# MLP up products by seven of eight block products, in turn with the preceding part's down products

## The chip, the cores and the metric

The kernel runs on one core of one Trainium2 chip. The metric is device time in microseconds of that core; a span is the time from the first to the last instruction of one profiled execution. A core has TensorE (matrix products into PSUM, eight banks of 512 float32 columns per partition), VectorE (DVE), ScalarE (ACT), GpSimd (POOL) and SyncE (SP, which here only starts DMAs). Each engine works through a queue of its own; they meet at semaphores.

## The reference

Two blocks follow each other on one sequence of 512 tokens with 1024 features, in float32. The first block has two layers, each a mixer (layer 0 a gated delta rule beside a short convolution, layer 1 a sparse attention) and an MLP:

```python
def squared_relu_mlp(h, w_up, w_down):
    return jnp.square(jax.nn.relu(h @ w_up)) @ w_down
...
    for layer in range(DEPTH):
        h = rms_norm(x, mix_norm[layer])
        ...
        x = x + squared_relu_mlp(rms_norm(x, mlp_norm[layer]), w_up[layer], w_down[layer])
    return rms_norm(x, final_norm)
```

`w_up` is 1024 x 4096, `w_down` 4096 x 1024. The second block (two layers of latent attention beside a Fourier branch) has no MLP. The change touches the two MLPs and what leads into them.

## The kernel before

**Layout.** Activations stand feature-major: a tile is 128 features (partitions) x 512 tokens; `x` has KT = 8 of them. A product keeps a 128 x 128 weight tile in TensorE and streams the tokens.

**Three passes.** To keep float32 precision, each operand is split into a high part (rounded to fp32r) and a low part (the rest), and `three` (L758) forms w_hi x_lo + w_lo x_hi + w_hi x_hi in PSUM. Each pass loads its weights anew. `gemm` (L764) runs 8 input tiles x 3 passes = 24 matmuls for one output tile of 128 x 512 in the MLP.

**Weights.** `stream_of` lays all weights out as 312 blocks of eight 128 x 128 tiles, in the order of use. SP loads block b into `raw[b % 3]` once POOL has finished the low part of block b - 3 (L2693 to L2699). ACT makes `w_hi` (`weights`, L1407 to L1416) once TensorE has used block b - 3, POOL makes `w_lo` (L2709), and TensorE waits for `w_lo_ready`. ACT's copies stand in its queue between its other work: each step of the program first calls `weights(block + 2)`. `plan_core` (L321) walks through the program once and gives every product its block, PSUM bank and use number, and every split its number; all engines wait by these numbers.

**MLP.** Four parts of 1024 hidden features. In each, eight up products (L831 to L837); for each, DVE takes relu times the root of the norm into `relu` (L2082), ACT squares it into `stage` (L1530) and makes `a_hi`, DVE makes `a_lo` (L2032). Then eight down products (L839), each added to `x` by DVE (`add_to_x`, L2074). Products turn through banks 0 to 3.

**Into the MLP.** The mixer's output products come first, eight tiles of `x`: of 12 matmuls each in layer 0 (blocks of two tiles), of 24 in layer 1. Per tile DVE adds it to `x`; ACT makes `h_hi` (L1493) and its square (L1489); DVE makes `h_lo` (L2038) and adds the square to the norm sum (L2053) (`sums_before_norm` L2062, `products_before_norm` L1509). The first up product waits for each input tile by itself. The norm sum goes through TensorE (`norm_sum`, L819) after that product, and ACT forms the root with Ln and Exp (`norm_root`, L1502), which only the relu needs.

## Time and profile before

| what | us |
|---|---|
| median of 3 runs | 2103.3 |
| lowest and highest of the 3 | 2093.99, 2109.73 |
| span of the profiled execution | 2099.7 |

Of the profiled execution the page gives the span alone; the time of a run has some microseconds around its span. Busy time of an engine is the union of its instructions. The marked time of a matmul holds its way through the array as well, so matmuls overlap in the record and the rate is read from their starts. Weight loads are a row of their own, PEld. In a row of a group, "idle before" is what the engine stood still ahead of its instructions, and the name after the arrow is what ended it. The record's clock row gives the granted clock as 1.00 of full speed for the span.

### The profile page before, as it was taken

The page shows a single profiled execution, that of the slowest core. Times are in us where ns is not written, and L with a number is a line of the kernel's source. Part 1 is how long each engine was busy: PE and PEld are TensorE (multiplying, and loading weights), DVE is VectorE, ACT ScalarE, POOL GpSimd, SP SyncE. Part 2 cuts the span into 40 slices and gives each one's busy share as a digit, 9 for nine tenths or more (in the row PEclk, how much of TensorE's full clock was granted, in tenths as well). Part 3 has the DMA queues.
Part 4 walks back from the last instruction along what each step waited for, and adds up shares of the span by engine and source line. Part 5 has one row for each costly group of instructions (what it writes and reads, how often), then busy time and mean ns, then how long its engine had stood idle before and what let it go on. Part 6 is the DMA issues. An engine that isn't in the chain of part 4 may idle for free.

```text
span 2099.7 us, 28844 instructions
## 1 busy us (share of the span) xinstructions
PE 2076.6 (99%) x11148; PEld 1645.5 (78%) x11148; DVE 947.6 (45%) x1431; ACT 933.3 (44%) x1477; POOL 759.2 (36%) x316
## 2 busy tenths in 40 slices
PE   8999999999999999999999999999999999999999
PEld 5777788888888886668888888778788887877887
DVE  7875552112137256765211212667733354773331
ACT  7642453323236326774322324556742344765231
POOL 3332144444444630003444444344034443402443
PEclk9999999999999999999999999999999999999999
DMA  4442133333332431002333333232022333201232
GB/s 155 134 123 70 45 104 99 92 101 91 94 99 88 146 96 31 2 14 92 100 91 101 91 101 101 74 97 81 12 81 90 91 93 94 85 22 61 91 100 81
DMA packets 62710, 178.96 MB, mean 85 GB/s; under 512 B 17776, under 2 KB 18160, under 8 KB 62592
## 3 DMA queue, kind: packets, MB, share of 16 engines
q1 hardware_dynamic: 47600, 168.04, 26.3%
q10 hardware_dynamic: 14992, 9.22, 1.6%
q8 instruction: 89, 1.46, 0.3%
q14 instruction: 29, 0.24, 0.0%
HBM read 171.97 MB, written 3.70 MB: 84 GB/s over the span
## 4 chain that ended last, share of the span: by engine, by line
issue 48%; PE 34%; POOL 16%; ACT 1%; POOLq 0%; DMA 0%; SPq 0%; DVE 0%
POOL w_lo L2709 16%; PE banks L760 9%; PE banks L762 9%; PE banks L761 9%; PE banks L1282 1%; PE banks L1295 1%; PE banks L1267 1%; PE banks L811 1%; PE banks L1273 1%; PE banks L1239 0%; DMA x<-in_x 0%; PE banks L1330 0%; POOLq L2715 0%; POOLq L2717 0%; PE banks L1331 0%
## 5 line engine op out<-in xcount | busy, mean ns | idle before, releaser
L2709 POOL TENSOR_TENSOR w_lo<-raw,w_hi 128x1024 fp32r<-128x1024 f32 (+1 forms) x312 | 759.0, 2434 | 1322.8 <-ACT w_hi L1415 1322.7
L760 PE MATMUL banks<-h_lo,w_hi 128*128 128x512 f32 (+1 forms) x1408 | 567.0, 403 | 9.3 <-POOL w_lo L2709 9.3
L762 PE MATMUL banks<-h_hi,w_hi 128*128 128x512 f32 (+1 forms) x1408 | 554.7, 394 | 0.0
L761 PE MATMUL banks<-h_hi,w_lo 128*128 128x512 f32 (+1 forms) x1408 | 551.5, 392 | 0.0
L1415 ACT ACTIVATE w_hi<-raw 128x1024 fp32r<-128x1024 f32 (+1 forms) x312 | 327.9, 1051 | 489.4 <-PE banks L762 456.5
L760 PEld LDWEIGHTS banks<-h_lo,w_hi 128*128 128x128 f32 (+1 forms) x1408 | 264.4, 188 | 73.8 <-POOL w_lo L2709 8.7
L761 PEld LDWEIGHTS banks<-h_hi,w_lo 128*128 128x128 f32 (+1 forms) x1408 | 264.5, 188 | 62.2 <-issue 4.8
L762 PEld LDWEIGHTS banks<-h_hi,w_hi 128*128 128x128 f32 (+1 forms) x1408 | 264.3, 188 | 60.7 <-issue 0.7
L760 PE MATMUL banks<-a_lo,w_hi 128*128 128x512 f32 x768 | 304.5, 397 | 0.0
L762 PE MATMUL banks<-a_hi,w_hi 128*128 128x512 f32 x768 | 301.6, 393 | 0.0
L761 PE MATMUL banks<-a_hi,w_lo 128*128 128x512 f32 x768 | 299.8, 390 | 0.0
L2074 DVE TENSOR_TENSOR x<-x,banks 128x512 f32<-128x512 f32 x104 | 71.4, 687 | 341.0 <-PE banks L762 341.0
L762 PEld LDWEIGHTS banks<-a_hi,w_hi 128*128 128x128 f32 x768 | 144.3, 188 | 33.4
L761 PEld LDWEIGHTS banks<-a_hi,w_lo 128*128 128x128 f32 x768 | 144.4, 188 | 33.0 <-issue 1.0
L760 PEld LDWEIGHTS banks<-a_lo,w_hi 128*128 128x128 f32 x768 | 144.5, 188 | 31.3 <-issue 1.3
L2082 DVE SCALAR_TENSOR_TENSOR relu<-banks,norm 128x512 f32<-128x512 f32 x64 | 44.3, 692 | 270.5 <-PE banks L762 259.8
L1530 ACT ACTIVATE stage<-relu 128x512 f32<-128x512 f32 x64 | 40.5, 632 | 208.7 <-DVE relu L2082 208.7
L2053 DVE TENSOR_TENSOR norm<-norm,sq 128x512 f32<-128x512 f32 x49 | 85.7, 1749 | 2.5 <-ACT sq L1489 1.2
L1973 ACT ACTIVATE sig<-sig,params 128x512 f32<-128x512 f32 x32 | 23.2, 726 | 140.6 <-DVE sig L2635 140.6
L2635 DVE TENSOR_TENSOR sig<-banks,norm 128x512 f32<-128x512 f32 x32 | 22.1, 692 | 111.6 <-PE banks L762 111.6
L1821 ACT ACTIVATE prob<-banks,nb 128x128 f32<-128x128 f32 (+3 forms) x128 | 66.2, 534 | 1.4 <-DVE nb L2452 1.4
L2032 DVE TENSOR_TENSOR a_lo<-stage,a_hi 128x512 fp32r<-128x512 f32 x84 | 61.6, 733 | 7.5 <-ACT a_hi L1478 7.3
(365 smaller groups left out, 2466.5 us busy)
## 6 DMA issues: line engine op xcount, KB each, us to landing
raw<-in_weights SPq DMA_DIRECT2D x311, 512.0 KB, 3.6
x<-in_x SPq DMA_DIRECT2D x4, 512.0 KB, 6.2
AT<-row_dram ACTq DMA_DIRECT2D x4, 512.0 KB, 7.6
out<-x SPq DMA_DIRECT2D x8, 256.0 KB, 2.6
eg<-row_dram ACTq DMA_DIRECT2D x8, 128.0 KB, 3.3
phase<-in_phase ACTq DMA_DIRECT2D x1, 706.0 KB, 4.9
phase<-in_phase ACTq DMA_DIRECT2D x1, 704.0 KB, 4.2
ld_dram<-Ld ACTq DMA_DIRECT2D x1, 512.0 KB, 5.4
```

The costliest lines, as they stand in the source:

```text
L760: mm(out, w_hi, x_lo, start=first, stop=False)
L761: mm(out, w_lo, x_hi, start=False, stop=False)
L762: return mm(out, w_hi, x_hi, start=False, stop=last)
L1415: f(c.w_hi[:, b % RING, 0:n], c.raw[:, b % RING, 0:n], ACT.Copy).then_inc(c.w_hi_ready, 1)
L1530: step(f(c.stage[:, split[key] % 3, :], c.relu[:, i % 2, :], ACT.Square))
L1821: ins = f(c.prob[:, i % 4, s, e], c.pairs[bank[key][0] // 2][:, s, e], ACT.Exp, bias=c.nb[:, i % 4, m:m + 1], accum_out=c.nb[:, i % 4, 4 + ...
L1973: f(gate, gate, ACT.Sigmoid, bias=pa["merge"][:, at:at + 1]).then_inc(c.sig_ready, 1)
L2032: tt_op(dst, stage(key, False), hi.bitcast(F32), ALU.subtract).then_inc(c.split_lo, 1)
L2053: tt_op(c.norm[:, slot, :], c.norm[:, slot, :], c.sq[:, i % 2, :], ALU.add).then_inc(c.norm_sum, 1)
L2074: tt_op(c.x[:, m, :], c.x[:, m, :], out[:, :], ALU.add).then_inc(release(key), 1)
L2082: stt(c.relu[:, i % 2, :], product(key)[:, :], 0.0, r, ALU.max, ALU.mult).then_inc(release(key), 1)
L2709: return nc.gpsimd.tensor_tensor(c.w_lo[:, slot, 0:n], c.raw[:, slot, 0:n], c.w_hi[:, slot, 0:n].bitcast(F32), ALU.subtract)
```

## The change

An up product of a 256-feature group `g` (of 512 in a part; eight parts now) is a matrix of 2 x 2 blocks times the input's 2 x 2 blocks (two feature tiles x two halves of the tokens). With sums of weight blocks and sums of input blocks made beforehand, seven block products take the place of eight, and seven to nine additions put the result together. So:

- A weight block holds one group's eight tiles for four input tiles (two pairs). ACT copies its W21 quarter to PSUM bank 4 (`w21`), DVE forms four sums in banks 4 and 5 (`weight_sums`), ACT makes their high part (`sums_hi`), DVE their low part (`weight_sums_lo`). W21's own high and low parts are not made; ACT's and POOL's work on such a block is three quarters.
- On the way in, input tiles go in pairs: ACT writes the gained tile to bank 6, DVE forms four sums in banks 6 and 7, and high and low parts follow (`pair_hi`, `input_sums`, `input_sums_hi`, `pair_lo`, `input_sums_lo`).
- `seven` issues per block 7 products x 2 pairs x 3 passes = 42 matmuls of 256 columns; two blocks make a group.
- ACT copies the first product (`first`), DVE adds the products up in PSUM, takes relu there, ACT squares from PSUM, DVE takes the low part from PSUM. `relu` is gone.
- The order on TensorE is: two up blocks, then (from the second part on) four down products of the preceding part, of 12 matmuls each, in banks 6 and 7 by turns. Each down product is added to `x`, now 64 per MLP.
- The loops of SP and POOL over the blocks are written out.

```diff
-FF_PARTS = 4
+FF_PARTS = 8
...
+    def by_pairs(w):
+        for first in range(0, w.shape[0] // P, 4):
+            for out, into in ((1, 0), (0, 0), (0, 1), (1, 1)):
+                for k in (first, first + 2):
+                    yield w[(k + into) * P:(k + into + 1) * P, out * P:(out + 1) * P]
+        for part in range(FF_PARTS + 1):
+            for g in range(2):
+                if part < FF_PARTS:
+                    add(by_pairs(up[:, (2 * part + g) * SUM_BLOCK:(2 * part + g + 1) * SUM_BLOCK]))
+                if part:
+                    add(out_major(down[(part - 1) * T:part * T, g * T:(g + 1) * T]))
...
+SEVEN = [("p1", W_11, X_11), ("p2", W_12, X_21), ("p6", W_S2, X_T2), ("p3", W_S4, X_22), ("p7", W_S3, X_T3),
+         ("p5", W_S1, X_T1), ("p4", W_22, X_T4)]
+SUM_BANKS, INPUT_BANKS, DOWN_BANKS = (4, 5), (6, 7), (6, 7)
...
+    def seven(layer, part, g, half, beside_products=None):
+        key, first = ("up", layer, part, g), part == g == 0
+        b = block[key][0] + half
+        i_sum = sum_blocks.index(b)
+        pe.wait_ge(c.w_lo_ready, b + 1)
+        pe.wait_ge(c.s_lo_ready, i_sum + 1)
...
+        for n, (_, w, x) in enumerate(SEVEN):
+            bnk, use, _ = bank[(*key, n // 2)]
...
+                if part and n % 4 == 0:
+                    before = (part, 0) if g else (part - 1, part > 1)
+                    pe.wait_ge(c.split_lo, split[("a", layer, before[0], 2 * before[1] + n // 4)] + 1)
+            if n == 2 and beside_products:
+                pe.wait_ge(c.split_lo, split[("ht", 2 * layer + 1, PAIRS - 1)] + 1)
+                beside_products()
+            for k in range(2):
+                i = 2 * half + k
+                if first:
+                    pe.wait_ge(c.split_lo, split[("ht" if x > X_22 else "hx", 2 * layer + 1, i)] + 1)
...
+                x_hi, x_lo = c.hs_hi[:, i, x, :], c.hs_lo[:, i, x, :]
+                mm(out, w_hi, x_lo, start=half == k == n % 2 == 0, stop=False, skip_group_check=True)
+                mm(out, w_lo, x_hi, start=False, stop=False, skip_group_check=True)
+                ins = mm(out, w_hi, x_hi, start=False, stop=half == k == 1, skip_group_check=True)
+            if n == len(SEVEN) - 1:
+                ins.then_inc(c.block_used, 1)
+            elif half and n % 2:
+                ins.then_inc(c.bank_filled[bnk], 1)
...
+    def down(layer, part, g):
+        if g == 0:
+            pe.wait_ge(c.split_lo, split[("a", layer, part, NT - 1)] + 1)
+        x_hi, x_lo = [tiles(t, NT, part % 2 * NT) for t in (c.a_hi, c.a_lo)]
+        for m in range(NT * g, NT * g + NT):
+            gemm(("down", layer, part, m), x_hi, x_lo, tile0=m % 2 * NT)
...
+        for part in range(FF_PARTS + 1):
+            for g in range(2):
+                if part < FF_PARTS:
+                    seven(layer, part, g, 0)
+                    seven(layer, part, g, 1, (lambda: norm_sum(2 * layer + 1)) if part == g == 0 else None)
+                if part:
+                    down(layer, part - 1, g)
...
+            if b in sums:
+                w21(b)
+                sums_hi(b)
+            cols = slice(SUM_BLOCK if b in sums else 0, n)
+            f(c.w_hi[:, b % RING, cols], c.raw[:, b % RING, cols], ACT.Copy).then_inc(c.w_hi_ready, 1)
...
+        if i:
+            act.wait_ge(c.s_lo_ready, i)
...
+        f(c.psum[SUM_BANKS[0]][:, 0:SUM_BLOCK], c.raw[:, b % RING, 0:SUM_BLOCK], ACT.Copy).then_inc(c.w21_ready, 1)
...
+        act.wait_ge(c.weight_sums, i + 1)
+        if i > 1:
+            act.wait_ge(c.block_used, sums[i - 2] + 1)
+        f(c.w_hi_s[:, i % 2, :], c.pairs[SUM_BANKS[0] // 2][:, :, :].rearrange("p b t -> p (b t)"), ACT.Copy).then_inc(c.s_hi_ready, 1)
...
+    def pair_hi(n, k):
+        x_final(act, c, bank, n, k)
+        i, gain = k // 2, norm_gain(c, pa, n, k)
+        if k % 2:
+            f(c.hs_hi[:, i, X_21:X_22 + 1, :].rearrange("p b t -> p (b t)"), c.x[:, k, :], ACT.Copy, scale=gain).then_inc(c.split_hi, 1)
+        else:
+            f(c.hs_hi[:, i, X_11, :], c.x[:, k, 0:HALF], ACT.Copy, scale=gain)
+            if i:
+                act.wait_ge(c.split_lo, split[("ht", n, i - 1)] + 1)
+            else:
...
+            f(c.psum[INPUT_BANKS[0]][:, :], c.x[:, k, :], ACT.Copy, scale=gain).then_inc(c.gained, 1)
+        norm_square(n, k)
+    def input_sums_hi(n, i):
+        act.wait_ge(c.t_ready, (n // 2) * PAIRS + i + 1)
+        f(c.hs_hi[:, i, X_T2:X_T3 + 1, :].rearrange("p b t -> p (b t)"),
+          c.pairs[INPUT_BANKS[0] // 2][:, :, :].rearrange("p b t -> p (b t)"), ACT.Copy).then_inc(c.split_hi, 1)
...
+        for m in range(KT):
+            passed(*key, m)
+            if m % 2 == 0 and m:
+                pair_hi(n, m - 1)
+                input_sums_hi(n, m // 2 - 1)
+            elif m:
+                pair_hi(n, m - 1)
+        pair_hi(n, KT - 1)
+        input_sums_hi(n, PAIRS - 1)
...
+        for n, ((part, g), ahead) in enumerate(up_cycles()):
+            key, after = ("up", layer, part, g), block[("up", layer, *ahead)][0] if ahead else None
+            down = block[("down", layer, part - 1, NT * g)][0] if part else None
+            if part:
+                weights(down)
+            if ahead:
+                w21(after)
+            if n == 0:
+                norm_root(2 * layer + 1)
+            if part:
+                weights(down + 1)
+            if ahead:
+                sums_hi(after)
+            f(c.first[:, n % 2, :], filled((*key, 0))[:, 0:HALF], ACT.Copy).then_inc(c.first_ready, 1)
+            if ahead:
+                w21(after + 1)
+                weights(after)
+            for i in range(2):
+                m, y = 2 * g + i, c.psum[bank[(*key, 2 * i)][0]]
+                act.wait_ge(c.relu_ready, (layer * FF_PARTS + part) * NT + m + 1)
+                f(c.a_hi[:, part % 2 * NT + m, :], y[:, :], ACT.Square)
+                f(y[:, :], y[:, :], ACT.Square).then_inc(c.split_hi, 1)
+            if ahead:
+                sums_hi(after + 1)
+                weights(after + 1)
+        products_before_norm((2, "final")[layer], "down", layer, FF_PARTS - 1)
...
+    def weight_sums(b):
...
+        dve.wait_ge(c.w21_ready, i + 1)
+        tt_op(s3, w11, s1, ALU.subtract)
+        first = marked(tt_op(s1, s1, w22, ALU.add))
+        after(first)
+        second = marked(tt_op(s2, s1, w11, ALU.subtract))
+        after(second)
+        tt_op(s4, w12, s2, ALU.subtract).then_inc(c.weight_sums, 1)
+    def weight_sums_lo(b):
+        i = sums.index(b)
+        dve.wait_ge(c.s_hi_ready, i + 1)
+        tt_op(c.w_lo_s[:, i % 2, :], c.pairs[SUM_BANKS[0] // 2][:, :, :].rearrange("p b t -> p (b t)"),
+              c.w_hi_s[:, i % 2, :].bitcast(F32), ALU.subtract).then_inc(c.s_lo_ready, 1)
...
+    def input_sums(n, i):
...
+        dve.wait_ge(c.gained, (n // 2) * PAIRS + i + 1)
+        t1 = marked(stt(d[:, left], x1[:, right], g1, b[:, left], ALU.mult, ALU.subtract))
+        stt(d[:, right], x2[:, right], g2, b[:, right], ALU.mult, ALU.subtract)
+        after(t1)
+        t2 = marked(stt(b[:, left], x2[:, right], g2, d[:, left], ALU.mult, ALU.subtract))
+        after(t2)
+        stt(b[:, right], x2[:, left], g2, b[:, left], ALU.mult, ALU.subtract).then_inc(c.t_ready, 1)
+    def pair_lo(n, i):
...
+            ALU.mult, ALU.subtract)
+        hi_part, lo_part = [t[:, i, X_21:X_22 + 1, :].rearrange("p b t -> p (b t)") for t in (c.hs_hi, c.hs_lo)]
+        stt(lo_part, c.x[:, 2 * i + 1, :], norm_gain(c, pa, n, 2 * i + 1), hi_part.bitcast(F32), ALU.mult, ALU.subtract)\
+            .then_inc(c.split_lo, 1)
+    def input_sums_lo(n, i):
...
+        tt_op(lo_part, c.pairs[INPUT_BANKS[0] // 2][:, :, :].rearrange("p b t -> p (b t)"), hi_part.bitcast(F32), ALU.subtract)\
+            .then_inc(c.split_lo, 1)
...
+    def sums_before_pairs(n, *key):
+        for m in range(KT):
+            b = block[(*key, m)][1] + 2
+            if b in sums and b > prepared:
+                weight_sums(b)
+                weight_sums_lo(b)
+                prepared = b
+            add_to_x((*key, m), m)
+            if m:
+                norm_add(n, m)
+            if m % 2:
+                input_sums(n, m // 2)
+            elif m:
+                pair_lo(n, m // 2 - 1)
+                input_sums_lo(n, m // 2 - 1)
+        norm_add(n, KT)
+        pair_lo(n, PAIRS - 1)
+        input_sums_lo(n, PAIRS - 1)
...
+        left, right = slice(0, HALF), slice(HALF, T)
+        for n, ((part, g), ahead) in enumerate(up_cycles()):
+            key, b = ("up", layer, part, g), block[("up", layer, *ahead)][0] if ahead else None
...
+            if ahead:
+                weight_sums(b)
+                weight_sums_lo(b)
+            dve.wait_ge(c.first_ready, (layer * FF_PARTS + part) * 2 + g + 1)
+            tt_op(bank_0[:, left], bank_0[:, right], first, ALU.add)
+            filled((*key, 1))
+            u2_done = marked(tt_op(u2, bank_1[:, left], first, ALU.add))
+            after(u2_done)
+            filled((*key, 2))
+            u3_done = marked(tt_op(u3, bank_2[:, left], u2, ALU.add))
+            u4_done = marked(tt_op(u4, bank_2[:, right], u2, ALU.add))
+            after(u3_done)
+            tt_op(bank_2[:, right], bank_2[:, right], u3, ALU.add)
+            after(u4_done)
+            tt_op(bank_0[:, right], bank_1[:, right], u4, ALU.add).then_inc(release((*key, 1)), 1)
+            dve.wait_ge(c.block_used, block[key][0] + 2)
+            tt_op(bank_2[:, left], bank_3[:, left], u3, ALU.add).then_inc(release((*key, 3)), 1)
+            if n == 0:
+                r = root(2 * layer + 1)
+            read((*key, 1))
+            stt(bank_0[:, :], bank_0[:, :], 0.0, r, ALU.max, ALU.mult).then_inc(c.relu_ready, 1)
+            read((*key, 3))
+            stt(bank_2[:, :], bank_2[:, :], 0.0, r, ALU.max, ALU.mult).then_inc(c.relu_ready, 1)
+            if part:
+                add_to_x(("down", layer, part - 1, NT * g), NT * g)
+            if ahead:
+                weight_sums(b + 1)
+            for i in range(2):
+                m, a = 2 * g + i, ("a", layer, part, 2 * g + i)
+                dve.wait_ge(c.split_hi, split[a] + 1)
+                at = part % 2 * NT + m
+                tt_op(c.a_lo[:, at, :], c.psum[bank[(*key, 2 * i)][0]][:, :], c.a_hi[:, at, :].bitcast(F32), ALU.subtract)\
+                    .then_inc(c.split_lo, 1)
+            if ahead:
+                weight_sums_lo(b + 1)
+            if part:
+                for m in range(NT * g + 1, NT * g + NT):
+                    add_to_x(("down", layer, part - 1, m), m)
+        sums_before_norm(next_norm, "down", layer, FF_PARTS - 1)
...
+            for b in range(n_blocks):
                 pool.wait_ge(c.w_hi_ready, b + 1)
+                low_part(b % RING, SUM_BLOCK if b in sums else 0, TILES * (P if b else AB_ROWS)).then_inc(c.w_lo_ready, 1)
```

The rest of the diff places the new tensors and semaphores and passes `sums`, the list of the blocks with sums, to the engines' programs. `up_banks` gives a group banks 0 to 3, and 6, 1, 7, 3 to the second group of the first part.

## Rows read from the trace of the kernel before

**Rows 1.** The page: busy time, share of the span and instructions of each engine

```profile
PE 2076.6 (99%) x11148; PEld 1645.5 (78%) x11148; DVE 947.6 (45%) x1431; ACT 933.3 (44%) x1477; POOL 759.2 (36%) x316
```

**Rows 2.** The waits: engine and line that waited, for whom; us, times, longest

```profile
PE banks L760 <- POOL w_lo L2709: 9.3, 2, 8.3
```

**Rows 3.** The timeline in an up product of MLP 0: start us, us, engine, line

```profile
500.25 0.39 PE L760 MATMUL banks<-h_lo,w_hi 128*128 128x512 f32 x1
500.26 0.19 PEld L761 LDWEIGHTS banks<-h_hi,w_lo 128*128 128x128 f32 x1
...
505.06 0.39 PE L760 MATMUL banks<-h_lo,w_hi 128*128 128x512 f32 x1
```

**Rows 4.** The timeline of transposes of 128 columns: matmuls, and their weight loads

```profile
1882.74 1.09 PE L1282 MATMUL banks<-common,prob 128*128 128x128 f32 x8
...
1882.74 0.85 PEld L1282 LDWEIGHTS banks<-common,prob 128*128 128x128 f32 x8 [0.37 <-issue]
```

**Rows 5.** The timeline of the compression products, 320 and 160 columns in turn

```profile
686.33 0.36 PE L1069 MATMUL banks<-kc,w_hi 128*128 128x320 f32 x1
...
686.52 0.25 PE L1071 MATMUL banks<-kc,w_lo 128*128 128x160 f32 x1
686.52 0.19 PEld L1069 LDWEIGHTS banks<-kc,w_hi 128*128 128x128 f32 x1
686.61 0.35 PE L1069 MATMUL banks<-kc,w_hi 128*128 128x320 f32 x1
...
687.68 0.35 PE L1069 MATMUL banks<-kc,w_hi 128*128 128x320 f32 x1
```

**Rows 6.** Groups by line and form: count | busy us, mean ns | idle before, releaser

```profile
L2074 DVE TENSOR_TENSOR x<-x,banks 128x512 f32<-128x512 f32 x104 | 71.4, 687 | 341.0 <-PE banks L762 341.0
...
L2599 DVE TENSOR_REDUCE nb<-banks 128x2 f32<-128x1024 f32 x32 | 39.1, 1221 | 13.4 <-PE banks L1273 13.4
...
L2621 DVE TENSOR_TENSOR d_lo<-banks,d_hi 128x256 fp32r<-128x256 f32 x16 | 6.6, 423 | 2.6 <-ACT d_hi L1962 2.5
...
L1814 ACT ACTIVATE probT<-banks 128x1024 f32<-128x1024 f32 x24 | 24.6, 1025 | 15.5 <-PE banks L1172 15.5
...
L1962 ACT ACTIVATE d_hi<-banks 128x256 fp32r<-128x256 f32 x16 | 6.1, 382 | 3.7 <-PE banks L1333 2.8 <-PE banks L1331 0.5
...
L2709 POOL TENSOR_TENSOR w_lo<-raw,w_hi 128x1024 fp32r<-128x1024 f32 x311 | 757.8, 2438 | 1316.2 <-ACT w_hi L1415 1316.1
```

**Rows 7.** The timeline of DVE, and one row of POOL, at the entry to MLP 0

```profile
277.81 0.69 DVE L2074 TENSOR_TENSOR x<-x,banks 128x512 f32<-128x512 f32 x1 [2.06 <-PE banks L762]
278.41 0.75 DVE L2038 SCALAR_TENSOR_TENSOR h_lo<-x,params,h_hi 128x512 fp32r<-128x512 f32 x1
...
284.56 2.90 DVE L2053 TENSOR_TENSOR norm<-norm,sq 128x512 f32<-128x512 f32 x1
...
295.20 0.68 DVE L2074 TENSOR_TENSOR x<-x,banks 128x512 f32<-128x512 f32 x1
...
297.06 0.74 DVE L2038 SCALAR_TENSOR_TENSOR h_lo<-x,params,h_hi 128x512 fp32r<-128x512 f32 x1
...
284.50 2.42 POOL L2709 TENSOR_TENSOR w_lo<-raw,w_hi 128x1024 fp32r<-128x1024 f32 x1 [3.08 <-ACT w_hi L1415]
```

**Rows 8.** The timeline of ACT at the entry to MLP 0: the root of the norm

```profile
298.12 1.28 ACT L1505 ACT_TABLE_LOAD   x1
...
302.64 0.63 ACT L1507 ACTIVATE norm<-norm 128x512 f32<-128x512 f32 x1
```

**Rows 9.** TensorE's first matmuls (timeline), and the window over them (busy, PEclk, DMA, GB/s)

```profile
8.31 0.65 PE L760 MATMUL banks<-h_lo,w_hi 128*40 128x512 f32 x1 [8.31 <-POOL w_lo L2709]
...
11.25 0.39 PE L761 MATMUL banks<-h_hi,w_lo 128*40 128x512 f32 x1
11.49 0.40 PE L762 MATMUL banks<-h_hi,w_hi 128*40 128x512 f32 x1
...
9.50:12.00 2.50, 2.50 (x9) 1.12 (x8) 2.48 (x5) 2.49 (x5) 0.00 (x0) 1.00 1.03 414
```

196 lines of the change are left out of this document (120 added, 76 removed).

## The prediction

> **What bounds the kernel now.** I read the busy times first: the matmuls cover 2076.6 of 2099.7 us, and VectorE (DVE), ScalarE (ACT) and GpSimd (POOL) are each under half busy [rows 1]. TensorE waited for another engine for only 9.3 us in two places, 8.3 of them at the start [rows 2]. Busy TensorE time overlaps, so the rate comes from the timeline: between 500.25 and 505.06 us lie 21 matmuls of 512 columns, 0.229 us each, each with its own weight load of 0.19 us beside it [rows 3]. The kernel is a stream of such pairs, and time goes only if the stream gets shorter and nothing opens a hole in it.
>
> **What the change does to the stream.** Up products before: 2 layers x 32 tiles x 8 x 3 = 1536 matmuls x 0.229 = 351.7 us. After: 2 layers x 16 (part, g) x 2 blocks x 7 x 2 x 3 = 2688 matmuls of 256 columns. The columns fall by an eighth, the matmuls rise by three quarters. The break-even is 351.7 / 2688 = 0.131 us a matmul. The down products stay 1536 matmuls.
>
> No row has a 256-column fp32r stream, so I bound it. From 512 columns: 512 / 2.4 = 213, so each matmul pays 16 ns besides its columns; 256 / 2.4 + 16 = 123 ns. The load alone is no longer than that: eight transposes of 128 columns, each with a full load, take (1.09 - 0.28) / 7 = 0.116 us each, and their loads come every (0.85 - 0.14) / 7 = 0.10 us [rows 4]; I take 0.11, between them, as the lower bound. The upper one is the compression stage, where matmuls of 320 and 160 columns alternate: five pairs from 686.33 to 687.68 take 0.270 each [rows 5]. That is 35 ns a matmul over its columns, so 142 ns at 256. But those rows also say where the excess sits: the load for the matmul after the short one starts at 686.52, with the short one, and the matmul it serves ends at 686.96, so it began near 686.96 - 0.18 - 0.13 = 686.65, 0.125 after its load began (0.18 is what a 512-column matmul's 0.39 has over its columns [rows 3]). A 256-column stream gives its load just that time. I take 0.124: 2688 x 0.124 = 333.3 us, a gain of 18.4. Ends: 0.11 gives 56 us gained, 0.142 gives 30 us lost.
>
> The page "TensorE: Matmul & The Clock Gate" of the Trainium skill (Back-to-back issue gap) has N / 2.4 + 2.5 ns, 109 ns at 256 columns and 216 at 512; at 512 the trace has 229 [rows 3], so the trace disagrees. By the page the up stream would be 293 us, 40 less than I take.
>
> **In a steady cycle.** A cycle is seven-product blocks U0, U1 (42 x 0.124 = 5.2 each) and four down products of 12 x 0.229 = 2.75. Durations I use: DVE on PSUM 0.69 for 512 columns, 0.42 for 256, 1.22 for 1024 (the nearest row is a reduction); ACT 1.03 for 1024, 0.38 for 256, and so 0.81 for 768; POOL 2.44 a full block, so 1.8 for three quarters [rows 6]. Queued work starts about 0.09 before the end of its forerunner (277.81 + 0.69, next at 278.41 [rows 7]). The DVE work of a cycle is then some 14 of 21.5 us, ACT 10, POOL 8: no bound. The tight place is bank 7, between down product m1 and m3. DVE may begin add(m0) 2.98 us into the down products (2.75 + 0.18 + hop), and has queued before add(m1): add 0.6, four sums 1.65 (two wait for their forerunner), two a_lo 1.2, low part of the sums 1.15, add 0.69: it frees the bank at 8.3, and TensorE wants it at 8.25. With a hop, 0.13 us lost x 28 cycles = 3.6 us. Range 0 to 0.6 a cycle (0 to 17 us). ACT's copy of the sums lies beside the a_lo pair. The weight DMAs keep their size and count and their wait for w_lo; SP and POOL queues are in the same block order. Nothing of this is worth time. The waits that are new: ACT's sums_hi for weight_sums, with w_hi, squares and `first` behind it; DVE's low part for that copy, with the adds, and so banks 6 and 7, behind it; TensorE for the low sums, made 5 us or more ahead here.
>
> **Entering MLP 0.** Before, each output product (2.75 us) asks DVE for an add, a low half and a norm add. The last add starts at 295.20, the last low half at 297.06, and TensorE, done at about 294.1, takes h tile by tile and loses nothing [rows 7]. After, the pairs come in turn through one pair of PSUM banks (6, 7). Per pair DVE has: 2 adds 1.2, 2 norm adds 1.2, four input sums 1.6, pair_lo 0.4 + 1.2, the low part of the sums 1.15: 6.8 us against 5.5 of TensorE. To that come operations with two SBUF inputs (norm_add, pair_lo) that meet a POOL block: one took 2.90 instead of 0.68 beside a POOL block begun at 284.50 [rows 7]. And two weight_sums + low parts, in which DVE waits for ACT's copy between: 3.9 each; and ACT's gained copy of a pair, which waits for the pair before. Stepping through both queues from add(m1) at 277.81: input sums of pair 0 end at 280.2, its low parts at 284.8 (with 0.7 for a meeting with POOL). norm_add(3) waits until 286.2, for ACT's square, which stands behind the gained copy, and that waits for the low part of pair 0. Input sums of pair 1 end at 288.4, the weight sums of the first up block at 290.1, ACT's copy at 291.2, their low part at 292.4, add(m4) at 293.0, norm_add, behind POOL's block, at 294.6, pair_lo at 296.2, the low part of pair 1 at 297.3. The same round takes pair 2 to 308.7 and 309.9 (low weights of the second block at 306.5), and pair 3 to 315.8 and 317. TensorE has 3 matmuls after 294.1, goes on at 296.2, ends the first block at 301, has 3 matmuls after 308.7 and goes on at 315.8. Unhindered it would stand there at 294.1 + 5.2 + 0.4 = 299.7. Loss 16.0 us; 8 if POOL and ACT never stand in the way (only the 6.8 - 5.5 per pair and the two sums), 22 if every such meeting costs.
>
> **Entering MLP 1.** Output products take 5.5 us, so DVE is near level until the sixth. Sums for the second block can start only after it, and the chain behind them (sums with copy 3.8, add 0.6, norm_add, input sums, norm_add, pair_lo) makes pair 3 ready 10.3 us after the last product; TensorE wants it at 5.4. Loss 4.9 (0 to 8).
>
> **First blocks of each MLP.** ACT has norm_root ahead of sums_hi(after). Ln and Exp, each with a table load of 1.28, take from 298.12 to 303.27 before, beside full up tiles [rows 8]. After, the square sum comes in the second block, and behind the Exp stand sums_hi 1.03, DVE's low part 1.15, w21 0.38, w_hi 0.81, POOL 1.8: block 3 is ready 4.6 us after block 2 ends. With no down products between, the next three blocks miss by 0.9, 0.6 and 1.7 (relu, sums, ACT copy, POOL are 5.5 to 7 us in series behind a 5.2 us block). 7.8 x 2 layers = 15.6 us (8 to 22).
>
> **The clock.** After the 8.3 us wait at the start, seven steps between matmuls of 512 columns take 8.31 to 11.25, 0.42 us each, the next takes 0.24 [rows 9]: 512 / 1.2 GHz is 0.43, so this is the lower of the clock's two levels, though the granted clock of the stretch is given as 1.00. It cost some 1.3 us. For holes of 4 to 7 us I take 3 us in all (0 to 8).
>
> **Leaving an MLP.** Its last eight products are 2.75 instead of 5.5 us. That is what layer 0's output products were before, and there TensorE lost nothing [rows 7]: 0.
>
> **Sum.** -18.4 + 3.6 + 16.0 + 4.9 + 15.6 + 3.0 = +24.7 on the span of 2099.7 = 2124.4. The median of the runs, 2103.3, is 3.6 above that span: 2128.
>
> **Rivals.**
> A, at the entries the pairs come in time: DVE gets through a pair in the 5.5 us of TensorE, since it does not stand behind POOL and ACT as I step it. The holes of both entries and their clock loss go: 2128 - 16.0 - 4.9 - 3.0 = 2104, no change. It is not slower from the point where all holes together stay under the 18.4 us of the stream. For it: DVE idles 2.06 us before the add at 277.81 [rows 7], and every engine but TensorE is under half busy [rows 1]. Against: the chain is serial through ACT and one PSUM pair.
> B, the weight load paces the stream at 0.11: 2128 - 38 = 2090, and with A 2066. For it speak the transposes [rows 4], against it the 16 ns that every 512-column matmul pays although its load is long done [rows 3]. The page's rule above gives nearly this.
> C, 256 columns behave as the mixed pairs [rows 5], 0.142 each: 18 ns x 2688 = 48 us more, 2176.
> D, bank 7 is late by 0.6 us or more in each of the 28 cycles: 13 us more or over, 2141. The point from which it decides: DVE's queue between add(m0) and add(m1) over 5.5 us.
> E, the change saves no TensorE time at all, since the interval is 0.131: 2146.
>
> **Chances.** Forecast 0.50 (its own range 2112 to 2143), A 0.19, B 0.05, C 0.07, D 0.12, E 0.07. A measurement of this kernel can tell about 1% (21 us) from no change. Slower by over 1% (above 2124) takes 0.28 of the forecast's 0.50 and C, D, E: 0.54. Faster by over 1% (under 2082) needs B and A together, or the other holes small as well as A's: 0.07. Between: 0.39. The range leaves out B and half of C: 2098 to 2160.
>
> **What would show it.** Right: 256-column matmuls start 0.122 to 0.126 apart inside a block; TensorE idle of 12 to 18 us around the second up block of layer 0, waiting for DVE hs_lo; a wait of some 5 us for POOL w_lo at the third block of each layer; DVE busy about 1280 us (14 us in 32 cycles and some 40 at the entries, for the 135 of relu, a_lo and adds). Wrong: an interval of 0.13 or more, or under 0.118; TensorE without holes at both entries; down products that wait for a bank by more than 0.5 us in each cycle.

## The result, and the profile after

The kernel after takes 2120.21 us (median of 4 runs, 2119.11 to 2122.73), the kernel before 2102.25 (4 runs): a ratio of 1.0088, 95% interval 1.0061 to 1.0114, 18 us slower. The profiled execution has a span of 2117.6 us against 2099.7. The prediction of 2128 us was 8 us high, on the right side, and inside its range; of its steps some were right, one was right in size but put the wait at the wrong place, and the gain of the stream was put at little more than half of the true one.

The page of the kernel after, its busy time and the slices of TensorE and its clock:

```profile
PE 2059.5 (97%) x12300; PEld 1683.4 (79%) x12300; DVE 1233.6 (58%) x2079; ACT 1013.9 (48%) x1653; POOL 722.3 (34%) x316
...
PE   8999978999999999999899999999999999999999
...
PEclk9999989999999999999899999999999999999999
```

Against [rows 1], TensorE is busy for 17 us less with 1152 matmuls more: the work did become cheaper. DVE gained 286 us and the span grew all the same. The 7 and the 8 in the sixth and seventh slice and the 8 in the twentieth are the entries of the two MLPs; the clock has its 8 at both, in the sixth slice and the twentieth.

The waits of TensorE over the whole span (against the single row in [rows 2]):

```profile
PE banks L933 <- DVE x L2270: 18.4, 2, 14.3
PE banks L933 <- POOL w_lo L3013: 14.0, 6, 4.5
...
PE banks L832 <- DVE x L2270: 4.3, 3, 1.5
```

L933 is the first matmul of a seven-product group, L832 that of a down product. 18.4 us are the two entries, 14.0 the first blocks of the two layers, 4.3 the first group of down products of each layer.

Where the 18 us went can be read from starts alone. An MLP's time is taken here from the start of the last matmul ahead of it to the start of its own last one. The timeline has these four in the kernel before:

```profile
293.85 0.39 PE L762 MATMUL banks<-a_hi,w_hi 128*128 128x512 f32 x1
...
646.28 0.39 PE L762 MATMUL banks<-a_hi,w_hi 128*128 128x512 f32 x1
...
985.43 0.39 PE L762 MATMUL banks<-a_hi,w_hi 128*128 128x512 f32 x1
...
1337.87 0.39 PE L762 MATMUL banks<-a_hi,w_hi 128*128 128x512 f32 x1
```

and in the kernel after, whose first one, at 295.89, is shown below:

```profile
660.79 0.39 PE L834 MATMUL banks<-a_hi,w_hi 128*128 128x512 f32 x1
...
999.94 0.39 PE L834 MATMUL banks<-a_hi,w_hi 128*128 128x512 f32 x1
...
1356.59 0.39 PE L834 MATMUL banks<-a_hi,w_hi 128*128 128x512 f32 x1
```

That is 352.4 us in both layers before, and 364.9 and 356.7 after. Ahead of the first MLP the kernel after is 2.0 us later, between the two equal, behind the second 0.8 us shorter. 12.5 + 4.2 + 2.0 - 0.8 = 17.9 us.

**The stream.** The timeline of one up block of the kernel after: the first product, the first of the four with weight sums, and one later among these.

```profile
471.41 0.28 PE L933 MATMUL banks<-hs_lo,w_hi 128*128 128x256 f32 x1
...
472.77 0.28 PE L933 MATMUL banks<-hs_lo,w_hi_s 128*128 128x256 f32 x1
...
474.93 0.28 PE L933 MATMUL banks<-hs_lo,w_hi_s 128*128 128x256 f32 x1
```

Between the first two rows lie 12 steps, 1.36 us, 0.113 each; between the last two 18 steps, 2.16 us, 0.120 each. The mean over all such steps between 380 and 640 us is 0.1181 and not the 0.124 that I took. 2688 x 0.1181 = 317.5 against 351.7: the stream gained 34 us, or 17.1 in each layer, and not 18.4 in all. So each MLP would have been 352.4 - 17.1 = 335.3 us, and holes and clock cost 29.6 us in layer 0 and 21.4 in layer 1.

**The entry to MLP 0.** The timeline of TensorE and DVE there:

```profile
295.89 0.40 PE L834 MATMUL banks<-a_hi,w_hi 128*128 128x512 f32 x1
296.10 0.74 DVE L2321 SCALAR_TENSOR_TENSOR hs_lo<-x,params,hs_hi 128x512 fp32r<-128x512 f32 x1
...
305.14 1.82 POOL L3013 TENSOR_TENSOR w_lo<-raw,w_hi 128x768 fp32r<-128x768 f32 x1 [9.91 <-ACT w_hi L1536]
...
307.82 0.74 DVE L2321 SCALAR_TENSOR_TENSOR hs_lo<-x,params,hs_hi 128x512 fp32r<-128x512 f32 x1
...
309.62 0.67 DVE L2270 TENSOR_TENSOR x<-x,banks 128x512 f32<-128x512 f32 x1
310.55 0.55 PE L933 MATMUL banks<-hs_lo,w_hi 128*128 128x256 f32 x1 [14.25 <-DVE x L2270]
...
314.31 0.74 DVE L2321 SCALAR_TENSOR_TENSOR hs_lo<-x,params,hs_hi 128x512 fp32r<-128x512 f32 x1
```

DVE does what the prediction stepped: the low parts of pair 1 end at 296.8 (I had 296.2), the second block's low weights done at 307.0 (306.5), pair 2 done at 308.6 (308.7), pair 3 at 315.1 (315.8). But TensorE stands still before the first block, not after it, and what ends the wait is an add to x. The up products of a seven-product group claim banks by number, the first one bank 0, and in bank 0 lay the mixer's last output product, whose add stands behind all of DVE's chain at 309.62. The kernel before took banks in turn, and its first up product got the one that had been free longest. So there is one hole of 14.65 us. In layer 1 the same happens with bank 1, behind the first two of the seven products (1001.46 to 1005.92, 4.46 us).

**The first blocks.** TensorE, ACT, DVE and POOL ahead of the third block of layer 0:

```profile
321.62 0.63 ACT L1653 ACTIVATE norm<-norm 128x512 f32<-128x512 f32 x1
322.16 1.01 ACT L1562 ACTIVATE w_hi_s<-banks 128x1024 fp32r<-128x1024 f32 x1
...
322.85 0.28 PE L935 MATMUL banks<-hs_hi,w_hi 128*128 128x256 f32 x1
...
324.84 0.83 ACT L1536 ACTIVATE w_hi<-raw 128x768 fp32r<-128x768 f32 x1
...
325.74 1.81 POOL L3013 TENSOR_TENSOR w_lo<-raw,w_hi 128x768 fp32r<-128x768 f32 x1 [18.79 <-ACT w_hi L1536]
...
327.60 0.42 PE L933 MATMUL banks<-hs_lo,w_hi 128*128 128x256 f32 x1 [4.47 <-POOL w_lo L3013]
```

4.75 us, then 0.94 ahead of the fifth block and 2.18 ahead of the sixth, with none ahead of the fourth: not quite the series 4.6, 0.9, 0.6, 1.7 of the prediction, but nearly its sum. Beyond these there is a wait of 1.74 us ahead of the fourth down product of the first group (1.84 and 1.89 us ahead of the third and fourth in layer 1) for an add to x. The fourth waits for bank 7, the place that the prediction named as tight, at 0.13 us a cycle.

**The clock.** The window that holds most of the first hole (busy time by engine, then granted clock, DMA share, GB/s):

```profile
300.50:314.20 13.70, 3.65 (x17) 3.69 (x18) 11.71 (x21) 7.33 (x11) 1.82 (x1) 0.50 0.12 38
```

The granted clock is the lower of its two levels, 1.2 GHz, from 300.5 to 314.2 us, after TensorE had stood still since 295.9; and again in five shorter stretches behind other holes (123.0 to 126.4, 327.8 to 331.2, 348.3 to 351.7, 1003.6 to 1010.5, 1020.7 to 1027.5). There the 256-column matmuls start 0.21 us apart. Counting half of TensorE's busy time in the five stretches that lie in the MLPs, it cost some 10 us, 5 in each. With 24.3 us of holes in layer 0 and 16.0 in layer 1 that makes 29 and 21 of the 29.6 and 21.4.

### The profile page after: what moved, and what is told of

It is laid out like the page before. It is cut to its first block, busy times and chain, and to the rows that moved or that the text cites. A ratio compares the mean times of both kernels' runs of the same rounds, so it can differ in the third digit from the quotient of the medians.

```text
span 2117.6 us, 30554 instructions
## 1 busy us (share of the span) xinstructions
PE 2059.5 (97%) x12300; PEld 1683.4 (79%) x12300; DVE 1233.6 (58%) x2079; ACT 1013.9 (48%) x1653; POOL 722.3 (34%) x316
## 4 chain that ended last, share of the span: by engine, by line
PE 86%; DVE 7%; ACT 3%; issue 2%; DMA 1%; POOL 0%; ACTq 0%; SPq 0%; DVEq 0%
PE banks L832 19%; PE banks L834 18%; PE banks L833 18%; PE banks L933 5%; PE banks L934 5%; PE banks L935 5%; PE banks L1276 2%; PE banks L1310 2%; PE banks L1289 2%; PE banks L1399 1%; PE banks L1412 1%; PE banks L1384 1%; PE banks L883 1%; DVE norm L2249 1%; PE banks L1390 1%
## 5 line engine op out<-in xcount | busy, mean ns | idle before, releaser
L3013 POOL TENSOR_TENSOR w_lo<-raw,w_hi 128x1024 fp32r<-128x1024 f32 (+2 forms) x312 | 722.1, 2316 | 1378.5 <-ACT w_hi L1536 1378.4
L1536 ACT ACTIVATE w_hi<-raw 128x1024 fp32r<-128x1024 f32 (+2 forms) x312 | 314.4, 1009 | 474.0 <-PE banks L834 321.1
L832 PE MATMUL banks<-h_lo,w_hi 128*128 128x512 f32 (+1 forms) x896 | 366.2, 409 | 8.7 <-POOL w_lo L3013 8.7
L834 PE MATMUL banks<-h_hi,w_hi 128*128 128x512 f32 (+1 forms) x896 | 354.9, 396 | 0.0
L833 PE MATMUL banks<-h_hi,w_lo 128*128 128x512 f32 (+1 forms) x896 | 353.5, 395 | 0.0
L832 PE MATMUL banks<-a_lo,w_hi 128*128 128x512 f32 x768 | 304.2, 396 | 4.3 <-DVE x L2270 4.3
L832 PEld LDWEIGHTS banks<-h_lo,w_hi 128*128 128x128 f32 (+1 forms) x896 | 168.8, 188 | 53.6 <-issue 9.0
L832 PEld LDWEIGHTS banks<-a_lo,w_hi 128*128 128x128 f32 x768 | 144.3, 188 | 42.2 <-DVE x L2270 11.3
L933 PE MATMUL banks<-hs_lo,w_hi_s 128*128 128x256 f32 x512 | 148.5, 290 | 4.2 <-DVE x L2270 4.2
L934 PE MATMUL banks<-hs_hi,w_lo_s 128*128 128x256 f32 x512 | 147.3, 288 | 0.0
L935 PE MATMUL banks<-hs_hi,w_hi_s 128*128 128x256 f32 x512 | 147.1, 287 | 0.0
L933 PE MATMUL banks<-hs_lo,w_hi 128*128 128x256 f32 x384 | 109.1, 284 | 28.2 <-DVE x L2270 14.3
L935 PE MATMUL banks<-hs_hi,w_hi 128*128 128x256 f32 x384 | 108.5, 283 | 0.0
```

The lines of the kernel that those rows point to most:

```text
L832: mm(out, w_hi, x_lo, start=first, stop=False)
L833: mm(out, w_lo, x_hi, start=False, stop=False)
L834: return mm(out, w_hi, x_hi, start=False, stop=last)
L933: mm(out, w_hi, x_lo, start=half == k == n % 2 == 0, stop=False, skip_group_check=True)
L934: mm(out, w_lo, x_hi, start=False, stop=False, skip_group_check=True)
L935: ins = mm(out, w_hi, x_hi, start=False, stop=half == k == 1, skip_group_check=True)
```

## The experiments

Two theories stood at the start. The first: the stream is 34 us shorter, and three separate things at the beginning of each MLP (the bank claim and the chain of pairs behind it; the queue order behind the root of the norm; the clock) cost 52. The second: one of them carries nearly all, and the others are its shadow. MLP 0 and MLP 1 below are the times as read above.

**Claims in turn.** The banks of the output products are shifted, so that the first bank of MLP 0 is the one that was filled longest ago:

```
+    turn[0] += 3
     for m in range(0, KT, 2):
         gemm([("out", 0, m), ("out", 0, m + 1)], 1, apart=True)
+    turn[0] -= 3
...
+    turn[0] += 2
     each("out", 1, n=KT)
+    turn[0] -= 2
```

> The output products before each MLP are shifted in bank order, so that the last one lands in bank 3 and not in the bank that the first up block claims first (0 in layer 0) or second (1 in layer 1). If the bank claim holds the first up block back, its first matmul comes at about 297 us instead of 310.5 in layer 0; the second block then waits for pair 3 until about 315, so only 3 us are won there, and about 2 in layer 1: 5 us less than the changed kernel, 2115. If the x pairs themselves are the cause, the first block starts where it did and the time stays at 2120.

Measured: ratio 1.0075, interval 1.0062 to 1.0088; MLP 0 365.2 us, MLP 1 357.1. The waits of TensorE from 290 to 365 us:

```profile
PE banks L937 <- DVE x L2274: 7.5, 3, 5.9
PE banks L937 <- POOL w_lo L3017: 7.0, 3, 4.5
PE banks L937 <- DVE hs_lo L2325: 2.7, 2, 2.5
```

The hole moved into the block and broke up: 6.2 us at bank 2 and 1.6 at bank 3, each still for an add to x, then 2.9 for pair 3. The MLP takes as long as without the edit. The bank claim is where most of the wait is seen, but the last wait of the entry, up to 316.3 us, is now for the low part of pair 3. What holds TensorE is DVE's queue, in which the adds stand among the pairs, as the prediction had it.

**Order of the queues.** ACT makes the sums and low weights of the next blocks ahead of the root of the norm and of the squares, DVE its weight sums ahead of the root:

```
-            if n == 0:
-                norm_root(2 * layer + 1)
...
+            else:
+                weights(after)
                 w21(after + 1)
+                if n == 0:
+                    norm_root(2 * layer + 1)
+                sums_hi(after + 1)
+                weights(after + 1)
```

> In the first two groups of each MLP the weights of the blocks ahead (w_hi, sums, their low parts) are prepared ahead of the root of the norm and of the relu. If the queue order on ACT and DVE makes the holes behind the second block (4.75 and 4.75 us), they shrink to about 0.5 each and the later ones (1 and 2 us) to 2 or less in all: 5 us less per layer, and two stretches of lower clock per layer go with them (1.7 us each): 16 us less, 2104. If only the chain is too long and the hole moves to the next block, the sum of the holes stays and so does 2120.

> Both edits. If the two causes are apart, their gains add: 5 + 16 = 21 us less, 2099. If the work that is brought forward collides with the entry, it is over 2105.

Measured: order alone 1.0037 (1.0024 to 1.005), MLP 0 360.4 and MLP 1 351.1, 4.5 and 5.6 us less than after; both edits 1.0031 (1.002 to 1.0042), 359.9 and 350.8. In layer 0 the third block's wait is gone, and the longest for low weights is 1.5 us, at the fourth block, where it was 4.5 (waits, 290 to 365 us, order alone), while the entry keeps its 14.3:

```profile
PE banks L933 <- DVE x L2275: 14.3, 1, 14.3
PE banks L933 <- POOL w_lo L3022: 3.5, 3, 1.5
```

So the queue behind the norm's root is a cost of its own, 10 us in the two layers together where 16 were expected, and no shadow of the entry. The claims add nothing to it.

**Work on zeros in the holes.** TensorE does 256-column matmuls on zeros, added into the open bank, where it would wait (124 beside the claims in turn; 118 beside the claims and the order):

```
+            if first and half == 0 and n in (4, 6):
+                filler(layer, "n%d" % n, out)
```

> The bank shift, and 256-column matmuls of zeros into the bank at hand while TensorE waits at the entries: 46 + 16 + 28 in layer 0, 10 + 24 in layer 1, sized at 0.118 us each to fit the holes. The result is unchanged. If the lower clock after a hole costs time of its own, the two stretches at the entries go and the time is about 4 us under the run with the bank shift alone (2 us in each layer). If it costs nothing, or zeros do not hold the clock up, the times are equal; if the fillers overrun the holes, it is slower by what they overrun.

> The claims in turn and the new order of the queues, as in the run with both, and beside them 120 matmuls of 256 columns on zeros in the holes of the two entries, sized to the holes of that run (46, 12 and 22 in layer 0; 12 and 26 in layer 1), so that TensorE stays busy while it waits. Theory (holes cost twice, once as idle time and once as a lower clock behind them): the lower clock from 303 to 320 us goes, which holds about 17 us of stream of which half is lost less the holes in it, so 3 to 6 us less than the run with both edits: span 2102 to 2105, median 2098 to 2101. Rival: the clock's fall costs nothing, since it lies in the holes: the same as that run within 2 us, or slower by the filler that overruns the holes.

Measured: 1.0031 (1.0021 to 1.0042) and 0.9982 (0.9973 to 0.9991). The granted clock in the window shown above is now 1.00 (first filler run):

```profile
300.50:314.20 13.70, 11.92 (x97) 11.10 (x96) 11.82 (x19) 9.15 (x13) 1.82 (x1) 1.00 0.12 39
```

The MLPs are 5.4 and 4.2 us shorter than with the claims alone, and 5.0 and 1.3 shorter than with claims and order. In spans it is 10.6 and 15.3 us, more than the clock could give. Part of it had another cause: in these two traces the matmuls with weight sums start 0.114 us apart, also far from any hole. The filler's 32 bytes of zeros had moved the region of the weight sums by 64 bytes in SBUF. This was tested by itself (the address, below).

**Less work for DVE at the entry.** Once the additions of the norm's squares ahead of the MLPs are cut to two columns, as shown, which leaves out most of the norm's sum; once they are given whole to POOL, without and with the two edits above:

```
-    def add_square(slot):
+    def add_square(slot, w=T):
...
-        tt_op(c.norm[:, slot, :], c.norm[:, slot, :], c.sq[:, i % 2, :], ALU.add).then_inc(c.norm_sum, 1)
+        tt_op(c.norm[:, slot, 0:w], c.norm[:, slot, 0:w], c.sq[:, i % 2, 0:w], ALU.add).then_inc(c.norm_sum, 1)
```

> The norm adds of the two MLP entries touch 2 columns instead of 512, which leaves most of the norm's sum out. DVE then has 7 x 0.5 us less in each entry and meets POOL less. If DVE's queue sets the entry, the first up block of layer 0 starts 5 to 8 us earlier and the run is about 8 us shorter. If the turn through ACT and the one PSUM pair sets it, less than 2 us.

> The same adds whole, but on POOL between its weight blocks, which is idle there. By DVE's queue: 5 to 8 us at the entry of layer 0, 1 to 3 in layer 1, and 1 us of clock: some 9 less, 1.0045 times before. If POOL's adds (1.2 us or more each) delay ACT's squares and the low parts of the weights, nothing or slower.

> Bank shift, order and POOL adds together. If they add: 1.0031 of the first two together less 9 us, 0.9987 times before, that is no slower than before for the first time. If the entry is then paced by ACT, 1.001 or more.

Measured: MLP 363.5 and 353.7 without the additions (one run, 2108.17 us beside 2102.15); on POOL 1.0058 (1.0041 to 1.0074), 363.9 and 353.0; with all three edits 1.002 (1.001 to 1.0031), 357.4 and 349.0, not the 0.9987 of gains that add. In layer 0 the longest wait falls from 14.3 to 11.6 us without them and to 13.2 on POOL, so these additions are 1 to 3 us of the entry. The rest is what stays in the queues, the serial chain through the one pair of banks among it; no run takes its parts away one by one.

**The price of a narrow matmul.** The second block of each group streams 192 columns in layer 0 and 128 in layer 1:

```
+            cols_n = (192, 128)[layer] if half else HALF
...
-                x_hi, x_lo = c.hs_hi[:, i, x, :], c.hs_lo[:, i, x, :]
+                x_hi, x_lo = c.hs_hi[:, i, x, 0:cols_n], c.hs_lo[:, i, x, 0:cols_n]
```

> The second block of every group streams 192 columns a matmul in layer 0 and 128 in layer 1 instead of 256; it leaves out those tokens' share of pairs 2 and 3. If the 0.118 us of the changed kernel is the pace of the weight loads, the narrowed blocks keep 0.110 to 0.118 us a matmul in both layers and the run is 0 to 10 us shorter. If it is columns plus a fixed 16 ns, they take 0.096 and 0.069, and the run is near 45 us shorter.

The timeline of TensorE in a narrowed block of either layer, in the second with the weight loads (PEld) at the block's beginning:

```profile
474.15 0.25 PE L934 MATMUL banks<-hs_lo,w_hi 128*128 128x192 f32 x1
...
475.25 0.27 PE L935 MATMUL banks<-hs_hi,w_lo 128*128 128x192 f32 x1
...
1145.25 0.22 PE L934 MATMUL banks<-hs_lo,w_hi 128*128 128x128 f32 x1
1145.26 0.19 PEld L935 LDWEIGHTS banks<-hs_hi,w_lo 128*128 128x128 f32 x1
1145.31 0.28 PE L935 MATMUL banks<-hs_hi,w_lo 128*128 128x128 f32 x1
1145.37 0.19 PEld L936 LDWEIGHTS banks<-hs_hi,w_hi 128*128 128x128 f32 x1
1145.42 0.27 PE L936 MATMUL banks<-hs_hi,w_hi 128*128 128x128 f32 x1
...
1146.43 0.28 PE L936 MATMUL banks<-hs_hi,w_hi 128*128 128x128 f32 x1
```

Ten steps of 192 columns take 1.10 us, nine of 128 take 1.01: 0.110 and 0.112, and over hundreds of them 0.111 and 0.110. A third of the columns less, from 192 to 128, changes nothing, so at these widths something else than the columns sets the pace, at 0.11 us. The rows speak for the weight load: the first 128-column matmul of the block is followed by the next after 0.06 us, and from then on matmuls start 0.11 apart, as the loads do all along. No run streams without loads, so this is read from the trace and not tested. It is rival B's price, and 256 columns stand just above it. The one run took 2104.71 us beside 2102.15, its MLPs 361.7 and 352.7: 3.2 and 4.0 us less than after, within the 0 to 10 expected.

**Parts 0 and 1 with eight products.** In each layer the first two parts are computed as before, with 512-column matmuls from the same tiles, which get room for the missing quarter. The input sums are made beside them, one pair at a time, in banks 4 and 5; the first weight sums come at the end of part 1.

```
+PLAIN = 2
-SUM_BANKS, INPUT_BANKS, DOWN_BANKS = (4, 5), (6, 7), (6, 7)
+SUM_BANKS, INPUT_BANKS, DOWN_BANKS = (4, 5), (4, 5), (6, 7)
...
+def pair_cycle(i):
+    return [(0, 0), (0, 1), (1, 0), (1, 0)][i]
...
+                if part < PLAIN:
+                    plain(layer, part, g, 0, parted("hx", 2 * layer + 1) if part == g == 0 else None)
+                    if part == g == 0:
+                        norm_sum(2 * layer + 1)
+                    plain(layer, part, g, 1)
```

> Of each layer's eight parts, parts 0 and 1 are computed with eight block products (512-column matmuls, as before), while the input sums are made beside them one pair at a time in banks 4 and 5; parts 2 to 7 use seven products. Theory (the loss sits at the entries: one pair of banks, the sum of squares behind a block, and the clock that falls with the holes; the seven products are otherwise cheaper than the eight by (0.229 x 1536 - 0.118 x 2688) = 34 us): six eighths of the 34 us stay, 25.5, and all holes at the entries and first blocks go, with their clock. Profiled span 2099.7 - 25.5 = 2074 +- 5, median about 2077, ratio to before 0.987 to 0.990; matmuls run without a gap above 1.2 us from the last output product to the third part. Rival: the seven-product cycles themselves lose time wherever they begin (their sums wait for engines that are late at the first seven blocks, whenever these are): the holes of 5 us and less reappear at the beginning of part 2, span 2085 to 2095. Second rival: the gain of 34 us was worked out wrong (it is only the busy time of TensorE that fell): the ratio stays at 1.00 or above.

Measured: 2071.18 us, ratio 0.9885, interval 0.9867 to 0.9902; MLP 0 340.8 us, MLP 1 340.9. The page, and the window in which the kernel after stood still, both without a gap:

```profile
PE 2046.9 (99%) x12012; PEld 1663.5 (80%) x12012; DVE 1182.4 (57%) x1943; ACT 995.3 (48%) x1613; POOL 732.1 (35%) x316
...
PEclk9999999999999999999999999999999999999999
```

```profile
296.30:310.50 14.20, 14.20 (x62) 11.32 (x61) 7.47 (x12) 10.53 (x15) 4.88 (x2) 1.00 0.24 75
```

352.4 - 340.8 = 11.6 us in layer 0 and 11.5 in layer 1, 23 in all, of the 25.5 that six eighths of the stream's gain make. The holes do not come back at part 2, so the loss sat in the beginning. What the seven-product cycles cost besides is some 2 us: in each of them the first step inside the down products is 0.30 us instead of 0.23. The edit takes several things off the entry at once: the pairs, the first weight sums in the same queue, the claims by number, the sums behind the norm's root. By themselves the claims gave nothing and the order 10 us; pairs and weight sums have no run of their own.

**The address of the weight sums.**

```
-    h, a, local = tail, tail + 32768, at
+    h, a, local = tail, tail + 32768, (at + 127) // 128 * 128
```

> The change as it is, with one edit: the region that begins with the weight sums (w_hi_s, w_lo_s) starts at a multiple of 128 bytes in each partition instead of 64 beyond one (97536 instead of 97472). Theory (found in the traces of the two runs with filler, whose 32 bytes of zeros moved that region by 64 bytes: the matmuls that load weights from w_hi_s and w_lo_s start 119 to 121 ns apart in the kernel after and 114 there, those that load from w_hi and w_lo, which lie at a multiple of 128, 115 in both): the sums' matmuls fall to 114 to 115 ns, 1536 x 5.5 ns = 8.4 us, so span near 2109 and median near 2112, and the holes at the entries stay as they were. Rival: the address has nothing to do with it (the filler kernels were faster because of the granted clock or the stage at 120 us): the sums' matmuls stay at 120 ns and the span at 2117 +- 4.

Measured: 2101.15 us, ratio 1.0005, interval 0.9996 to 1.0014, with this one line. The same three rows of an up block:

```profile
467.51 0.28 PE L933 MATMUL banks<-hs_lo,w_hi 128*128 128x256 f32 x1
...
468.87 0.28 PE L933 MATMUL banks<-hs_lo,w_hi_s 128*128 128x256 f32 x1
...
471.59 0.28 PE L933 MATMUL banks<-hs_lo,w_hi 128*128 128x256 f32 x1
```

12 steps in 1.36 us and 24 in 2.72, 0.113 each: the sums' matmuls fell from 0.120 to 0.113. The MLPs are 2.0 and 3.0 us shorter, not the 8 that the steps add up to. In layer 0 the starts show where the gain went: the holes there add up to 3 us more than after, most of it in waits for DVE among the first down products; in layer 1 they are as long as they were, and about 1 us is open. The span fell by 15.0, and 10 of these have nothing to do with the MLP: ahead of the first one it is 4.7 us earlier, and from the second one's last matmul to the end, in code that no edit touches, it is 755.7 us instead of 761.1. The first of these is a hole of 3.2 us at 118.6 us, in which TensorE waits for DVE's work in the mixer and a square of ACT behind it, with a stretch of the lower clock after it. The window there, after and with this edit:

```profile
116.00:124.00 8.00, 5.20 (x20) 3.63 (x19) 7.52 (x18) 7.92 (x11) 0.80 (x1) 0.94 0.00 0
```

```profile
116.00:124.00 8.00, 8.00 (x33) 5.90 (x32) 7.52 (x18) 6.75 (x9) 3.55 (x2) 1.00 0.08 18
```

It is there in all traces with the old address, that of the kernel before too (2.4 us), and in none of the four with the new one; how the address closes it is not shown. The time behind the second MLP is 760.8 to 761.9 us in six traces with the old address, and 754.3 to 754.4 in four others with it. From 200 to 360 us behind it the 512-column matmuls start 0.2333 us apart in the six and 0.2289 in the four, by the same code and addresses. What sets that is open, and 5 to 7 us of a difference between two single profiles may be this alone. The profiles of the kernels before and after are both among the six, so their 18 us are free of it; that of the run with parts 0 and 1 plain is among the four, and its gain is the 23 us of the MLPs.

**Both, with the tail moved too.** Parts 0 and 1 with eight products; the sums' region and the tail, where the tiles hs, a and h lie, at a multiple of 128 bytes:

```
-    tail = (top - 2 * 32768) // 64 * 64
+    tail = (top - 2 * 32768) // 128 * 128
```

> Parts 0 and 1 with eight products, as in the run before, and both the region of the weight sums and the tail (the pairs' tiles hs, a and h) at multiples of 128 bytes (they stood 64 beyond one). Theory of the weights' address: 1152 matmuls with weight sums fall by 5.5 ns, 6.3 us, median 2071.2 - 6.3 = 2065, ratio to before 0.984 to 0.987. If the address of the moving operand counts too, the 512-column matmuls start less than 0.229 us apart, and the median is below 2060. Rival: no effect of addresses, the ratio stays at 0.9885 within 0.001.

Measured: 2063.94 us (2063.84 to 2064.18), ratio 0.9822, interval 0.9808 to 0.9835, the best version, 37 us under the kernel before and by the two ratios some 55 under the kernel after. The number came as expected, but not by the way expected. The same three rows:

```profile
462.54 0.28 PE L961 MATMUL banks<-hs_lo,w_hi 128*128 128x256 f32 x1
...
463.98 0.28 PE L961 MATMUL banks<-hs_lo,w_hi_s 128*128 128x256 f32 x1
...
466.82 0.28 PE L961 MATMUL banks<-hs_lo,w_hi 128*128 128x256 f32 x1
```

12 steps in 1.44 us, 24 in 2.84: 0.120 and 0.118. Moving hs undid what moving the sums had done, and slowed the other products as well; the MLPs stayed at 340.9 us each. The gain of 7 us came from the stage ahead of the first MLP (3.2), the mixer between (1.5) and behind (2.2). Moving the sums' region and not the tail, with parts 0 and 1 plain, wasn't tried.

## Why the prediction was right, and where it was wrong

**The stream.** This is the term that was mis-sized: "I take 0.124: 2688 x 0.124 = 333.3 us, a gain of 18.4". It was 0.118 and 34. The 16 ns that a 512-column matmul pays over its columns were carried over to 256 columns. 256 columns at 2.4 GHz are 107 ns, so in the good placement 7 to 9 ns are paid there, in the bad one 13. The lower end, 0.11 from the transposes [rows 4], is what the narrower matmuls then took, and the measured rate lay between it and the value taken. The mixed pairs of [rows 5] said nothing about a uniform stream. The page "TensorE: Matmul & The Clock Gate" of the Trainium skill (Back-to-back issue gap) gives N / 2.4 + 2.5 ns, 109 ns here, for a matmul by itself, and says that in a stream the load counts too, which the prediction's sentence on the page left out. No run reaches 109 at 256 columns, the best has 113.

**The entry to MLP 0.** Loss 16.0 forecast, 14.65 measured, and the queues of DVE and ACT ran as stepped, to within 1 us at each pair. The step that failed is "goes on at 296.2, ends the first block at 301": TensorE did not go on, since its bank was held by the last output product. Claims in turn showed that this costs nothing beyond the chain. Cutting or moving the norm's additions moved little (1.4 and 1.0 us of MLP 0, 3.0 and 3.7 of MLP 1); running parts 0 and 1 plain, with pairs and weight sums off the path, took the hole away. How the two share it is open. **MLP 1:** 4.9 forecast, 4.46 measured, again at the bank.

**The first blocks.** 7.8 us a layer forecast; 7.9 and 7.8 measured up to the sixth block, in three waits and not four, and 1.7 and 3.7 more in the first group of down products, which the prediction missed. Putting the sums and low weights ahead of the norm's root gave back 10 us in two layers, clock included, which shows the cause that was named.

**A steady cycle.** 3.6 us forecast for bank 7. The steady cycles lose about 2 us in both layers together, and not there: it is the longer first step inside the down products, 0.30 us. Apart from the first cycles TensorE did not wait for bank 7.

**The clock.** 3 us forecast, 10 counted, in five stretches. But holding the clock up with filler made the MLPs only about 4.5 us and 1 us shorter than what the address explains. Much of the lower clock lies in holes or ahead of the next wait for DVE, which probably comes at the same time whatever TensorE's speed. Counting half of the busy time of such a stretch then overstates what it costs.

**In sum**, forecast -18.4 + 3.6 + 16.0 + 4.9 + 15.6 + 3.0 = 24.7; measured about -34.2 + 2 + 14.7 + 4.5 + 21.1 + 10 = 18.1, where the MLPs grew by 12.5 + 4.2 = 16.7. (Each hole, counted from start to start, holds a step that the stream has anyway, 1.6 us in all.) The span grew by 1.2 us more outside the MLPs, 17.9, of which the prediction had nothing. The stream's error of 16 us was met by 7 of the clock and 5.5 of the first blocks on the other side. The forecast was near partly because two errors cancelled. Of the signs named beforehand, the wait of 5 us for low weights at the third block came; the interval did not (0.118, at the edge of the sign of being wrong), the hole stood ahead of the first block and not around the second, and DVE was busy for 1234 us and not 1280. Of the rivals, A was refuted (the pairs didn't come in time), C, D and E as well; B held in half: there is a floor at 0.11, seen at 192 and 128 columns, and the stream ran 3 to 9% above it.

## What to carry to other kernels

A cheaper inner scheme has a start: before moving a kernel to it, ask what must be ready for its first block, on which engine, and behind what. Here running the first quarter by the old scheme while the new one's operands were made turned 17 us of loss in the two MLPs into 23 of gain, where mending the queues one place at a time came back to about even. When an edit gains more than its theory allows, look for what else it moved: 32 bytes of zeros moved a region, changed the matmul rate and hid as a clock effect.

## What the runs showed of the hardware

- At 192 and 128 columns fp32r matmuls, each with its own 128x128 weight load, start 0.110 to 0.112 us apart, alike at both.
- At 256 columns the rate hangs on where weights and moving operand lie in SBUF: 0.113 to 0.116 with the weights at a multiple of 128 bytes and the moving tile 64 beyond one, 0.120 with both 64 beyond, 0.118 to 0.120 with both at a multiple. What they share to get in each other's way is not shown.
- The same 512-column matmuls behind the second MLP start 0.2333 us apart in six traces and 0.2289 in seven, four of them with the same addresses as the six.
- 512-column matmuls went from 0.2293 to 0.2280 us apart (mean over 450 to 750 us of the two kernels with plain parts 0 and 1) when the tail moved to a multiple of 128.
- Behind the holes at the entries and first blocks the granted clock was at the lower level in stretches of 3.4 to 13.7 us; matmuls on zeros in the holes of the first entry kept it up there.
